# Retention scores and value products: 16 fp32 products a head turned into 48 fp32r products, with their steps moved

## The reference, cut to what matters

```python
q_r = apply_rope(to_heads(rq, RET_HEADS), cos, sin) * (RET_DK ** -0.5)
k_r = apply_rope(to_heads(rk, RET_HEADS), cos, sin)
...
scores = jnp.einsum('bhid,bhjd->bhij', qc, kc) * decay[..., 0]
o = (jnp.einsum('bhij,bhjv->bhiv', scores, vc)
     + jnp.einsum('bhid,bhdv->bhiv', qc * jnp.exp(b), s))
...
o_r = merge_heads(head_layer_norm(o_r)) * ret_gn * jax.nn.silu(rg.astype(f32))
```

## Time and profile before

| | |
|---|---|
| median of 3 runs | 1720.34 us (1716.08 to 1720.62) |
| profiled execution | 1717.64 us, of which the profile's span is 1715.6 us |
| PE busy | 98% of the span |
| DVE busy, ACT busy | 59%, 43% |
| granted TensorE clock, mean | 0.998 of full speed |
| one pass of a head's 16 steps | 60.9 us, four of them from 544.0 to 787.6 us |

### The profile page before, as it was taken

The page is one execution under the profiler, slowest core; times in us unless marked ns, Lnnn a source line. Parts: engine busy times, 40 slices in busy tenths (PEclk is TensorE's granted clock), DMA queues, the critical chain, the costliest instruction groups (busy, mean ns, idle before and its releaser), DMA issues.

```text
span 1715.6 us, 21804 instructions
## 1 busy us (share of the span) xinstructions
PE 1686.9 (98%) x8069; PEld 1357.4 (79%) x8069; DVE 1011.1 (59%) x1153; ACT 743.1 (43%) x835; POOL 165.3 (10%) x177
## 2 busy tenths in 40 slices
PE   6999999999999999999999999999999999999998
PEld 2457788888878888888888788888888888888886
DVE  2445776777966777666665764445444454544444
ACT  3324222227555454445546654444444444343442
POOL 0011000000056355320000000000000000000000
PEclk9999999999999999999999999999999999999999
DMA  9998999999988666646676576666666666766662
GB/s 366 377 383 305 336 353 334 348 349 350 381 294 266 211 206 207 205 152 225 223 269 214 175 232 186 192 186 189 188 187 191 186 191 186 265 191 194 194 193 91
DMA packets 183612, 419.28 MB, mean 244 GB/s; under 512 B 12928, under 2 KB 13296, under 8 KB 173696
## 3 DMA queue, kind: packets, MB, share of 16 engines
q1 hardware_dynamic: 167680, 375.45, 66.4%
q0 software_dynamic: 7120, 27.64, 4.9%
q10 hardware_dynamic: 8752, 15.38, 2.4%
HBM read 397.92 MB, written 20.50 MB: 244 GB/s over the span
## 4 chain that ended last, share of the span: by engine, by line
PE 93%; DMA 4%; DVE 2%; issue 1%; ACT 0%; POOL 0%; SPq 0%; DVEq 0%; POOLq 0%; ACTq 0%
PE ps L1667 27%; PE ps L1679 27%; PE ps L1671 27%; PE ps L1749 2%; PE ps L1723 2%; DMA raw<-in_w_mod 2%; DMA wm<-in_w_mod 2%; PE ps L1765 1%; PE ps L1971 1%; PE ps L1955 1%; PE ps L2009 1%; DVE acc L1075 1%; PE ps L1896 0%; PE ps L2087 0%; PE ps L2074 0%
## 5 line engine op out<-in xcount | busy, mean ns | idle before, releaser
L1063 DVE TENSOR_TENSOR w_lo<-raw,w_hi 128x1024 fp32r<-128x1024 f32 x486 | 601.1, 1239 | 498.9 <-ACT w_hi L654 498.4
L654 ACT ACTIVATE w_hi<-raw 128x1024 fp32r<-128x1024 f32 x488 | 516.7, 1061 | 788.3 <-PE ps L1679 774.1
L1667 PE MATMUL ps<-w_hi,h_hi 128*128 128x512 f32 x1440 | 452.5, 394 | 0.3 <-issue 0.3
L1671 PE MATMUL ps<-w_hi,h_lo 128*128 128x512 f32 x1440 | 445.2, 389 | 0.0
L1679 PE MATMUL ps<-w_lo,h_hi 128*128 128x512 f32 x1440 | 392.5, 389 | 1.9 <-DVE w_lo L1063 1.9
L1679 PEld LDWEIGHTS ps<-w_lo,h_hi 128*128 128x128 f32 x1440 | 270.1, 188 | 58.5 <-DVE w_lo L1063 2.3
L1671 PEld LDWEIGHTS ps<-w_hi,h_lo 128*128 128x128 f32 x1440 | 270.3, 188 | 56.9
L1667 PEld LDWEIGHTS ps<-w_hi,h_hi 128*128 128x128 f32 x1440 | 266.9, 188 | 54.9 <-issue 1.5
L1075 DVE SCALAR_TENSOR_TENSOR acc<-wm,csil,acc 128x2048 f32<-128x2048 f32 x60 | 141.1, 2352 | 61.2 <-DMA wm<-in_w_mod 61.0
L1667 PE MATMUL ps<-w_hi,hid_hi 128*128 128x512 f32 x352 | 109.7, 389 | 0.0
L1671 PE MATMUL ps<-w_hi,hid_lo 128*128 128x512 f32 x352 | 109.7, 389 | 0.0
(11 more groups left out here) (315 smaller groups left out, 1377.8 us busy)
## 6 DMA issues: line engine op xcount, KB each, us to landing
raw<-in_w_in SPq DMA_DIRECT2D x184, 512.0 KB, 6.5
wm<-in_w_mod SPq DMA_DIRECT2D x64, 1024.0 KB, 7.1
raw<-in_ffn_w_gate SPq DMA_DIRECT2D x88, 512.0 KB, 4.3
raw<-in_ffn_w_up SPq DMA_DIRECT2D x88, 512.0 KB, 4.4
raw<-in_ffn_w_down SPq DMA_DIRECT2D x88, 512.0 KB, 4.7
raw<-in_w_mod SPq DMA_DIRECT2D x64, 512.0 KB, 8.1
raw<-in_w_out SPq DMA_DIRECT2D x32, 512.0 KB, 4.8
px<-stage ACTq DMA_DIRECT2D x44, 256.0 KB, 6.0
```

Of the source, the lines that this page charges most:

```text
L654: act.activation(w_hi[:, j % SPLIT, :, :], raw[:, j % RAW, :, :], ACT.Copy).then_inc(w_high, 1)
L1063: dve.tensor_tensor(w_lo[:, j % SPLIT, :, :], raw[:, j % RAW, :, :], w_hi[:, j % SPLIT, :, :].bitcast(F32), ALU.subtract).then_inc(w_low, 1)
L1667: pe.matmul(o, hi[:, kk, c], w_h[:, e, :], start=kk == 0, stop=False)
L1671: pe.matmul(o, lo[:, kk, c], w_h[:, e, :], start=False, stop=False)
```

## The change

The retention scores and value products are each done as three fp32r passes in place of fp32: 24 products of 256 columns for 8, twice a head. For that `r_qt`, `r_kt`, `r_v` and `r_a` get a high part, copied by ACT, and a low part, subtracted by DVE. ACT gains the copies `r_v_hi` (step 7) and `r_a_hi` (step 10); `r_qt` and `r_kt` were copied before and now are fp32r. DVE gains five low parts: context keys in step 4, queries and keys in step 7 behind `weigh`, values in step 8, `r_a_lo` in step 11. The low parts stand where `r_q`, `r_k`, `r_kc`, `r_v` and `r_a` stood, so POOL loads the next head's `r_q`, `r_k` and `r_kc` only after the value products.

The steps move: PE's scores from 7 to 9, DVE's decay from 8 to 10, PE's value products from 9 to 11, DVE's retention statistics from 10 to 12 and its normalization from 12 to 13. `pick_far` goes from 10 to 9. GLA's gating and transposes go ahead of retention's (DVE 12, PE 13, DVE 14 against 13, 14, 15). PE's wait in step 6 is now for DVE's low part of the context keys.

```diff
-                        act.activation(r_kt[:, 2:4, :], bank(4).rearrange("p (f n) -> p f n", f=2), ACT.Copy)\
-                            .then_inc(S("r_qkt_ready"), 1)
+                            .then_inc(S("r_high"), 1)
                         level_exp(i, 1)
+                    if p == 7:
+                        act.wait_ge(S("r_v_landed"), i * 32 + 32)
+                        act.activation(r_v_hi[:, :, :], r_v[:, :, :], ACT.Copy).then_inc(S("r_high"), 1)
...
                     if p == 10:
+                        act.wait_ge(S("r_a_ready"), i + 1)
+                        act.activation(r_a_hi[:, :, :], r_a[:, :, :], ACT.Copy).then_inc(S("r_high"), 1)
                         act.wait_ge(S("gates_landed"), i * 32 + 32)
                         act.activation(g_g[:, :, :], g_g[:, :, :], ACT.Silu).then_inc(S("g_silu"), 1)
...
+                    if p == 4:
+                        dve.wait_ge(S("r_high"), i * 5 + 1)
+                        dve.tensor_tensor(r_kt_lo[:, 2:4, :], bank(4).rearrange("p (f n) -> p f n", f=2),
+                                          r_kt[:, 0:2, :].bitcast(F32), ALU.subtract).then_inc(S("r_low"), 1)
                     if p == 7:
                         weigh(i, 1)
+                        dve.wait_ge(S("r_high"), i * 5 + 3)
+                        dve.scalar_tensor_tensor(out=r_qt_lo[:, :, :], in0=bank(5).rearrange("p (f n) -> p f n", f=2),
+                                                 scalar=RDK ** -0.5, in1=r_qt[:, :, :].bitcast(F32),
+                                                 op0=ALU.mult, op1=ALU.subtract).then_inc(S("r_low"), 1)
+                        dve.tensor_tensor(r_kt_lo[:, 0:2, :], bank(4).rearrange("p (f n) -> p f n", f=2),
+                                          r_kt[:, 2:4, :].bitcast(F32), ALU.subtract).then_inc(S("r_low"), 1)
                     if p == 8:
+                        dve.wait_ge(S("r_high"), i * 5 + 4)
+                        dve.tensor_tensor(r_v_lo[:, :, :], r_v[:, :, :], r_v_hi[:, :, :].bitcast(F32), ALU.subtract)\
+                            .then_inc(S("r_low"), 1)
+                    if p == 9:
+                        pick_far(i)
+                    if p == 10:
                         dve.wait_ge(S("r_scores_done"), i + 1)
...
                     if p == 11:
+                        dve.wait_ge(S("r_high"), i * 5 + 5)
+                        dve.tensor_tensor(r_a_lo[:, :, :], r_a[:, :, :], r_a_hi[:, :, :].bitcast(F32), ALU.subtract)\
+                            .then_inc(S("r_low"), 1)
                         dve.wait_ge(S("g_o_done"), i + 1)
...
+                if p == 9:
+                    pe.wait_ge(S("r_low"), i * 5 + 3)
+                    for a in range(4):
+                        o = bank(4, 2)[:, a * L:(a + 1) * L]
+                        c = slice((a % 2) * P, (a % 2 + 1) * P)
+                        for f in range(2):
+                            k_hi, k_lo = 2 * (a // 2) + f, 2 * (1 - a // 2) + f
+                            pe.matmul(o, r_kt[:, k_hi, c], r_qt[:, f, :], start=f == 0, stop=False)
+                            pe.matmul(o, r_kt[:, k_hi, c], r_qt_lo[:, f, :], start=False, stop=False)
+                            last = pe.matmul(o, r_kt_lo[:, k_lo, c], r_qt[:, f, :], start=False, stop=f == 1)
+                    last.then_inc(S("r_scores_done"), 1)
...
-                if p == 9:
-                    pe.wait_ge(S("r_a_ready"), i + 1)
-                    pe.wait_ge(S("r_v_landed"), i * 32 + 32)
+                if p == 11:
+                    pe.wait_ge(S("r_low"), i * 5 + 5)
                     for m in range(MT):
+                        o = bank(4)[:, m * RDK:(m + 1) * RDK]
                         for a in range(4):
-                            last = pe.matmul(bank(4)[:, m * RDK:(m + 1) * RDK], r_a[:, a, m * P:(m + 1) * P],
-                                             r_v[:, a, :], start=a == 0, stop=a == 3)
+                            c = slice(m * P, (m + 1) * P)
+                            pe.matmul(o, r_a_hi[:, a, c], r_v_hi[:, a, :], start=a == 0, stop=False)
+                            pe.matmul(o, r_a_hi[:, a, c], r_v_lo[:, a, :], start=False, stop=False)
+                            last = pe.matmul(o, r_a_lo[:, a, c], r_v_hi[:, a, :], start=False, stop=a == 3)
```

More of the change, by code:

```diff
@@ L187, in build @@
         r_tmp = reg("r_tmp", [P, 4, MT, P], 12)
-        r_qt = reg("r_qt", [P, 2, L], 16)
-        r_kt = reg("r_kt", [P, 4, L], 18)
+        r_qt = reg("r_qt", [P, 2, L], 16, F32R)
+        r_kt = reg("r_kt", [P, 4, L], 18, F32R)
+        r_qt_lo = reg("r_qt_lo", [P, 2, L], 0, F32R)
+        r_kt_lo = reg("r_kt_lo", [P, 4, L], 2, F32R)
+        r_v_hi = at("r_v_hi", [P, 4, RDK], F32R, ctx_w1_off)
+        r_v_lo = reg("r_v_lo", [P, 4, RDK], 6, F32R)
+        r_a_hi = reg("r_a_hi", [P, 4, L], 12, F32R)
+        r_a_lo = reg("r_a_lo", [P, 4, L], 22, F32R)
         r_a = reg("r_a", [P, 4, L], 22)
@@ L1388, in head @@
                     if p == 12:
+                        dve.wait_ge(S("r_o_done"), i + 1)
+                        for m in range(MT):
+                            dve.bn_stats(stats[:, 0, m, :], bank(4)[:, m * RDK:(m + 1) * RDK]).then_inc(S("r_stat"), 1)
+                        dve.wait_ge(S("r_stat"), i * 4 + 2)
+                        hold(8)
+                        for m in range(MT):
+                            dve.bn_aggr(mv[:, 0, m, :], stats[:, 0, m, :]).then_inc(S("r_stat"), 1)
+                        dve.wait_ge(S("r_stat"), i * 4 + 4)
+                        dve.tensor_scalar(mv[:, 0, :, 1:2], mv[:, 0, :, 1:2], EPS, None, ALU.add)\
+                            .then_inc(S("r_var_ready"), 1)
+                        dve.wait_ge(S("g_rstd_ready"), i + 1)
+                        dve.wait_ge(S("g_silu"), i + 1)
+                        for m in range(MT):
+                            last = dve.scalar_tensor_tensor(out=g_g[:, m, :], in0=bank(6)[:, m * GDV:(m + 1) * GDV],
+                                                            scalar=hr[:, 1, m, :], in1=g_g[:, m, :],
+                                                            op0=ALU.mult, op1=ALU.mult)
+                        last.then_inc(S("g_on_ready"), 1)
+                    if p == 13:
                         dve.wait_ge(S("r_silu"), i + 1)
@@ L1398, in head @@
                         last.then_inc(S("r_on_ready"), 1)
[L1399 to L1406, removed]
-                    if p == 14:
+                    if p == 14:
+                        dve.wait_ge(S("g_on_turned"), i + 1)
+                        dve.tensor_tensor(o_t[:, 1, bass.ds(i * 2, 2), :], bank(7).rearrange("p (a n) -> p a n", a=2),
+                                          cols[:, bass.ds(i * 2 + 72, 2)].rearrange("p (a o) -> p a o", o=1)
+                                          .broadcast_to([P, 2, L]), ALU.mult).then_inc(S("gla_head_done"), 1)
+                    if p == 15:
                         dve.wait_ge(S("r_on_turned"), i + 1)
@@ L1932, in at_head @@
                     pe.wait_ge(S("ret_head_done"), i + 1)
-                    pe.wait_ge(S("r_kct_ready"), i + 1)
+                    pe.wait_ge(S("r_low"), i * 5 + 1)
                     for b, t in ((5, r_q), (4, r_k)):
```

30 lines of the change are left out of this document (12 added, 18 removed).

## The result

The changed kernel takes 1725.49 us (median of 7 runs, 1723.75 to 1729.38), against 1716.54 us (1716.08 to 1720.62) for the kernel before, run beside it. The ratio is 1.0042 with a 95% interval of 1.0031 to 1.0053, so it is slower by 5.3 to 9.1 us, just past the 0.3% that counts as a difference here. The forecast was 1724.6 us in a range of 1714 to 1733.

The account below looks back on a forecast made before the run. PE, busy 98% of the span, was taken to bound the kernel: 5.9 us less PE work and 10.2 us of gaps at step 8 give +4.3 us, on the 1720.3 us median 1724.6 us, range 1714 to 1733.

Parts of the forecast that it names:

- The saving: Scores and value products in the four head passes: PE's work falls by 1.49 us a head, 5.9 us in all.
- the gap: PE waits at step 8 for DVE's `weigh`: 2.35 us a head, 3.1 in the first, 10.2 in all.
- I take 0.1134: Scores and value products: each 256-column fp32r product costs 0.1134 us, half a 512-column one; 48 cost 5.44 us a head.
- the restart: PE at step 8 after `weigh`: 0.19 us of weight load plus 0.06 for the semaphore before its first product.
- the low part of step 4: DVE's context keys' low part, ahead of the exponents, delays the first head's chain by 0.63 us; hidden in other heads.
- The clock: Rival: the wait at step 8 lowers PE's clock in each head, 4 x 1.8 = 7.2 us more, 1731.8 us; chance 5%.
- the side that I gave 0.44: Whole kernel: the chance given to it being slower by over 0.3%, above 1725.5 us, was 0.44.
- What was costed at nothing: Added DVE, ACT and POOL work beside PE: no wait, with `r_a_lo` done 0.7 us before PE reaches step 11.
- step 8 would not wait: Rival: `weigh` comes early enough for PE at step 8, leaving only the saved PE work: 1714.4 us; chance 9%.
- step 11 waits too: Rival: `r_a_lo` comes late, so PE waits 1 us a head at step 11: 1728.6 us; chance 16%.
- weight loads show: Rival: weight loads set each 256-column product at 0.188 us, 14.3 us more over 192 products: 1738.9 us; chance 11%.
- The fp32 price: Rival: fp32r products of 256 columns cost 0.433 us as in fp32, 55 us more in all: 1776 us; chance 2%.

Follow-up runs that it names:

- experiment 3: Changed kernel with 8 fp32 products in place of each 24 fp32r ones, low parts made but left out of the result: 1733.05 us, ratio 1.0083.
- experiment 4: Changed kernel with DVE's `weigh` moved behind the two low parts of step 7, so PE waits longer at step 8: 1734.07 us, ratio 1.0088.
- experiment 5: Changed kernel with PE doing nine unused 512-column products ahead of its wait in step 8: 1723.11 us, ratio 1.0023.
- experiment 1: Changed kernel with DVE's `weigh` in step 6, ahead of its split of slot 6, not in step 7: 1718.18 us, ratio 0.9993.
- 2: Changed kernel with `weigh` in step 6 and ACT's table load and silu moved from step 10 to 11: 1714.14 us, ratio 0.9977.
- 7: Changed kernel with `weigh` in step 6, silu in step 11, and fp32 products without the low parts in place of fp32r: 1719.85 us, ratio 1.0006.
- experiments 6: Changed kernel run again unchanged, for a second profile of its clock: 1727.0 us, ratio 1.0043.

## Why the prediction came out as it did

**The saving was over-sized, the gap too, and the errors cancel.** The step "I take 0.1134" is the first that was off: a 256-column fp32r product costs 0.119 us, so the saving is 4.8 us and not 5.9. It costs a little over half of a 512-column one, nowhere near the 0.188 of the load's record. The gap was forecast at 2.35 us a head and 3.1 in the first; it is 2.24 and 2.46, 9.1 in place of 10.2. In the later heads chain, place and releaser were as argued, and the wait was as long: `weigh` ends at 638.44, 2.10 behind slot 4. What was too long was the restart, 0.25 by a weight load and 0.06 for the semaphore; no row shows the 0.06, and PE starts 0.14 behind `weigh`. In the first the low part of step 4 was to delay the exponents by 0.63 us. They are only 0.12 later: the last one starts at 568.18 against 565.98, of which 2.08 is the later start of the whole stretch. DVE's two splits around the low part took 1.77 and 1.21 us, where they had taken 3.45 together before, and that makes up for most of it; why they were quicker is open. Both sums give +4.3, and that they agree is luck. So is part of the absolute time, 1724.6 forecast and 1725.49 measured: I added to 1720.34, the median of three runs, and seven runs beside the changed kernel have 1716.54. The change itself was forecast at +4.3 and is +7.2 by the ratio.

**The clock is the step that failed.** It was a rival with 5%, priced at 1.8 us a head in all heads, and put aside because "PE is dense on both sides of the wait". That is no protection. Experiments 3 and 4 show it in every head, experiment 5 that it goes when PE is kept busy, and 1, 2 and 7 that it did not come in twelve heads without the gap. A fall costs 1.5 to 1.6 us. In the changed kernel it is neither all nor none: one head of four in both profiles. The ratio's 7.2 us, less 4.3 for gaps and products and 0.4 for step 8, leave room for one or two falls in an execution (0.4 to 2.8 by the interval). The medians of experiments 6 and 5 differ by 3.9 us, which is some two and a half. That is argued from times, since the other executions have no trace. The change without the falls is nearest to experiment 5's 1.0023, inside the 0.3%; the falls carry it over, to the side that I gave 0.44.

**What was costed at nothing was close to it.** `r_a_lo` was to be 0.7 us ahead of PE; it is done at 654.14, PE's product starts at 654.64, so 0.5. DVE and ACT are busy for 48.2 and 31.4 us of a pass, as forecast. No wait for POOL's later loads shows in any head. What the prediction left out is the 0.10 us by which step 8 itself became longer; its reason is open.

**The rivals.** That step 8 would not wait is refuted by its row. That step 11 waits too did not happen, but experiment 1 shows how near it was. That weight loads show is refuted: full 128-row products with new weights each came every 0.120 us, beside load records of 0.19. The rule of the Trainium skill (TensorE: Matmul & The Clock Gate, "What overlaps and what doesn't") gave an estimated 0.22; for these products the trace does not agree with it. The fp32 price did not come either: by the 0.433 us an fp32 product costs, the 1776 us of that rival had left out the gap, and would have been 1786.

## What to carry to other kernels

When a step that covers a chain is moved, price the chain against what is left in front of it: here 3.47 us of scores left and 2.24 of them came back as a wait, more than the three passes save. The repair was one line, `weigh` ahead of a split. It brought the changed kernel back to the time of the one before; for it to come out below, the next wait in line (`r_a_lo`, half a microsecond away) had to be moved as well, and even then the gain is 0.23%. A short wait of TensorE can cost more than its length, so look at the granted clock and at the distance of products behind it, head by head and not in an average over the span.

## What the runs showed of the hardware

- Waits of 2.00 to 2.30 us in dense work were followed by a stretch of TensorE at its lower level: in one of four heads in two profiles of the changed kernel, and in four of four in experiment 3 with waits of the same length. What decides it at this length is open; it was not tried further. With waits of up to 3.5 us (experiment 4) it came in all four.
- The clock need not be down at the restart: in the first head of the changed kernel step 8 still ran as fast as in the second head (575.02 to 576.43 against 638.58 to 639.98) and the first two products of slot 5 nearly so (0.62 us against 0.57), and the slow ones begin about 2 us behind the restart. In other heads the slow stretch came sooner: in the first head of experiment 3 step 8 took 1.65 us in place of 1.41 (571.00 to 572.65), in that of experiment 4 1.98 (574.20 to 576.18).
- An fp32r product of 256 columns costs 0.118 to 0.120 us with a new weight load in front of each, an fp32 one 0.433 us, so three passes take 0.36 us, 17% less than one fp32 product.
